# The entry of a one-core decoder trunk: one queue for x and the first two weight tiles, and both tiles taken for each piece of x

## The chip, the cores and the metric

One Trainium2 chip, one core of it. The metric is the device time of one execution in microseconds (us). Three runs of the kernel before gave 826.4, 827.03 and 827.82; their median is 827.03. One further execution was profiled, and all rows of the profile come from it.

TensorE does the matmuls, ScalarE (ACT in rows) and VectorE (DVE) prepare operands and read results, GpSimd (POOL) does small work, and SyncE (SP) issues nearly all transfers.

## The reference, cut to what matters

```python
SEQ, D_MODEL, DEPTH = 256, 1024, 2
for l in range(DEPTH):
    xn = rms_norm(x, norm_mix_g[l])
    proj = xn @ w_in[l]
    xa, q, k, v, zc, xd = jnp.split(proj, splits, axis=-1)
    q = rope(q.reshape(B, S, ATT_HEADS, HEAD_DIM), positions)
    k = rope(k.reshape(B, S, ATT_HEADS, HEAD_DIM), positions)
    ...
    x = x + merged.astype(x.dtype) @ w_o[l]
    hn = rms_norm(x, norm_ffn_g[l])
    gu = hn @ w_ffn_in[l]
    x = x + (jax.nn.silu(gu[..., :FF_DIM]) * gu[..., FF_DIM:]) @ w_ffn_out[l]
return rms_norm(x, final_norm_g)
```

x is 256 tokens by 1024 channels, in float32. Four token mixers (pooling, attention, spatial gating, convolution) stand between `proj` and `merged`; the change does not touch them.

## The kernel before

**Products of two halves.** Every float32 weight tile and every activation is split into a high part (`w_hi`, `act_hi`, a float32r copy made by ScalarE) and a low part (`w_lo`, `act_lo`, the difference, made by VectorE). A product then takes three matmuls: hi x hi, hi x lo, lo x hi. A weight tile ("unit") holds 1 MB. The first units are columns of `w_in`: 1024 rows (8 blocks of 128, called k 0 to 7) by 256 columns. A unit is 48 matmuls of 256 columns: two column halves, eight k, three products.

**The ring.** `RING` is 3: three buffers each of `raw`, `w_hi` and `w_lo`; unit u uses buffer u % 3. SP loads unit u + 3 into `raw` when VectorE has finished the low part of unit u (`lo_ready`); ScalarE copies it to `w_hi` when TensorE has used that buffer (`w_used`), VectorE forms `w_lo`, and TensorE starts on it. Each engine runs its own list of instructions in order; semaphores tie them together.

**The norm.** xn's factor 1/rms does not go into the activations. TensorE works on x times the gains, and the factor is applied to results. ScalarE squares x (`first_norm`), VectorE adds the squares (`square_sum`), TensorE sums over the partitions (`norm_stat`, line 1105, after unit 2 in the first layer), VectorE computes the root and a diagonal (`norm_scale`, lines 1472 to 1476, ready: `diag_ready`), and TensorE spreads it (`norm_rms`, line 1115) after unit 3 and ahead of unit 4.

**The entry**, which the change rewrites. x comes in four pieces x0 to x3 of 256 channels (`load_x`, 256 KB each) and units 0 and 1 in four quarters of two k each (`load_quarter`, 256 KB each; quarter i of unit 0 is called q0i, of unit 1 q1i); unit 2 comes in two halves of 512 KB (lines 489). SP issues q00, x1, q01, x3, q03, then q10 to q13, the halves of unit 2, the positions and `ifreq`. ScalarE's queue issues the gains, x0, x2 and q02. TensorE turns a piece of x by four transposes (`first_x`, line 1252; x0's k 1 is turned a second time into another bank, line 1257), ScalarE multiplies it by the gains into `act_hi` (line 843) and VectorE forms `act_lo` (line 1769). Quarters are split on ScalarE (line 643, a helper that all copies share) and VectorE (line 1751).

TensorE's order before: 34 warm-up matmuls on zeros (`warm`), the turning of the gains (line 1278), x0, x1, 6 warm-ups, k 0 of unit 0, x2, k 1 of unit 0, x3, quarters 1 to 3 of unit 0, all of unit 1, unit 2, and so on. VectorE's order before: q00, x0, x1, q01, q02, x2, q03, x3, q10 to q13, the halves of unit 2, the position steps (lines 1806 to 1812: positions times frequencies, in turns), the sums of squares, the split of unit 3, the split of unit 4, `norm_scale`, `reduce_angles`, the split of unit 5. ScalarE takes the quarters and pieces in the same order, then the squares, one piece of x kept, and the splits of units 3, 4 and 5 as they land.

Lines 967 to 969 and 1012 to 1014 are the three matmuls of a product; line 1433 is VectorE's split of a whole unit, line 429 SP's load of one.

Of the kernel before, what the change touches and what calls it, by code (L numbers as in the profile page):

```python
# [124 lines left out]
def build(nc, T, out, inv_freq, inv_count):  # L125
# [10 lines left out]
    with ExitStack() as ctx:  # L136
# [287 lines left out]
        def _(sp):  # L424
# [51 lines left out]
                else:  # L476
                    load(l, slot, use, down(l, j), n=D)

            load_quarter(sp, 0, 0)
            load_x(sp, 1)  # L480
            load_quarter(sp, 0, 1)
            load_x(sp, 3)
            load_quarter(sp, 0, 3)
            for i in range(4):
                load_quarter(sp, 1, i)
            c0, w_rows = W_IN_UNITS[2][1], T["w_in"][0].rearrange("(k p) n -> p k n", p=P)
            for h, landed in enumerate((half_in, raw_full[2])):
# [140 lines left out]
        def _(act):  # L628
            act.dma_start(gain_rows[0:L * KT, :], T["norm_mix_g"].rearrange("l (r p) -> (l r) p", p=P))\
                .then_inc(gain_in, 16)  # L630
            load_x(act, 0)
            load_x(act, 2)
            load_quarter(act, 0, 2)

            for s in (1, 2):
                act.sem_inc(lo_ready[s], 1)
# [194 lines left out]
            def quarter(u, i):  # L831
# [2 lines left out]
                copy(kview(w_hi[u])[:, 2 * i:2 * i + 2, :], kview(raw[u])[:, 2 * i:2 * i + 2, :])\  # L834
                    .then_inc(quarter_hi[u] if i < 3 else hi_ready[u], 1)

            def first_x(i):
                act.wait_ge(xt_done, i + 1)
                for f in range(2):
                    k = 2 * i + f  # L840
                    if k == 1:
                        act.wait_ge(turned_again, 1)
                    last = nc.scalar.activation(act_hi[:, k, :], first_turned(k), ACT.Copy, scale=gains[:, k:k + 1])
                    if k == 0:
                        last.then_inc(first_hi, 1)
                last.then_inc(act_hi_ready, 1)

            def unit2_halves():
                hi = kview(w_hi[2])
# [5 lines left out]

            act.wait_ge(pre_const, 4)
            copy(junk[:, 0, 0:1], ones[:, 0:1])
            quarter(0, 0)
            act.wait_ge(gains_ready, 1)
            first_x(0)  # L860
            first_x(1)
            quarter(0, 1)
            for i in (2, 3):
                quarter(0, i)
                first_x(i)
            for i in range(4):
                quarter(1, i)
            unit2_halves()

# [94 lines left out]
        def _(pe):  # L964
# [296 lines left out]
            def quarter(u, i):  # L1261
                if i < 3:
                    pe.wait_ge(quarter_lo[u], i + 1)
                else:
                    weights(0, u, 0)
                if (u, i) == (0, 0):
                    pe.wait_ge(first_lo, 1)
                    unit_pair(0, 0, (0,))
                    first_x(2)
                    pe.wait_ge(act_lo_ready, 1)  # L1270
                    return unit_pair(0, 0, (1,))
                return unit_pair(u, u, (2 * i, 2 * i + 1))

            pe.wait_ge(pre_const, 1)
            warm(34)
            pe.wait_ge(pre_const, 3)
            pe.wait_ge(gain_in, 16)
            nc.tensor.transpose(bank[0][:, 0:L * KT], gain_rows[0:L * KT, :], ident[0:L * KT, 0:L * KT])\
                .then_inc(pre_pe, 1)
            first_x(0)  # L1280
            first_x(1)
            warm(6)
            pe.wait_ge(gains_ready, 1)
            for i in range(4):
                if i == 1:
                    first_x(3)
                if i > 0:
                    pe.wait_ge(act_lo_ready, i + 1)
                last = quarter(0, i)
            last.then_inc(w_used[0], 1)  # L1290
            pe.wait_ge(pre_const, 6)

            for l in range(L):
                for u in range(U_WO):
                    if l == 0 and u < 2:
                        if u == 1:
                            for i in range(4):
                                last = quarter(1, i)
                            last.then_inc(w_used[1], 1)
                            misc(l, u)  # L1300
                        continue
                    weights(l, u % RING, u // RING)
                    if u == 7:
# [94 lines left out]
        def _(dve):  # L1398
# [358 lines left out]
            def chain(ins):  # L1757
                turn[0] += 1
                ins.then_inc(turns_chain, 1)
                dve.wait_ge(turns_chain, turn[0])  # L1760

            def first_x(i):
                for f in range(2):
                    k = 2 * i + f
                    if k == 0:
                        dve.wait_ge(first_hi, 1)
                    else:
                        dve.wait_ge(act_hi_ready, i + 1)
                    last = V.scalar_tensor_tensor(act_lo[:, k, :], first_turned(k), gains[:, k:k + 1],
                                                  act_hi[:, k, :].bitcast(F32), ALU.mult, ALU.subtract)  # L1770
                    if k == 0:
                        last.then_inc(first_lo, 1)
                last.then_inc(act_lo_ready, 1)

            def unit2_halves():
                hi, lo, whole = kview(w_hi[2]), kview(w_lo[2]), kview(raw[2])
# [3 lines left out]
                V.tensor_tensor(lo[:, 4:8, :], whole[:, 4:8, :], hi[:, 4:8, :].bitcast(F32), ALU.subtract)\  # L1780
                    .then_inc(lo_ready[2], 1)

            quarter(0, 0)
            first_x(0)
            first_x(1)
            quarter(0, 1)
            for i in (2, 3):
                quarter(0, i)
                first_x(i)
            for i in range(4):  # L1790
                quarter(1, i)
            def reduce_angles():
# [12 lines left out]
            dve.wait_ge(pos_in, 16)  # L1805
            chain(V.tensor_copy(posf[:, 0, :], pos_i))
            dve.wait_ge(ifreq_in, 16)
            chain(V.tensor_scalar(ang[:, 0, :], posf[:, 0, :], ifreq[:, 0:1], None, ALU.mult))
            V.tensor_scalar(turns[:, 0, :], ang[:, 0, :], 1.0 / (2 * np.pi), None, ALU.mult)
            chain(V.tensor_scalar(turns[:, 1, :], ang[:, 0, :], 1.0 / (2 * np.pi), 0.25, ALU.mult, ALU.add))  # L1810
            chain(V.tensor_scalar(turns, turns, magic, None, ALU.add))
            chain(V.tensor_scalar(turns, turns, magic, None, ALU.subtract))
            dve.wait_ge(pre_const, 6)

            for i in range(1, 4):
                square_sum(0, 0, i)

            for l in range(L):
                if l > 0:
# [9 lines left out]
                        square_sum(l, 0, i)  # L1829
                    split(l, 2, 0)  # L1830
                for u in range(U_FFN):
                    if u == 1 + (l == 0):
                        norm_scale(l, 0)
                    if l == 0 and u == 2:
                        reduce_angles()
                    misc(l, u)
                    merge(l, u)
                    if u != U_WO + 2:
                        split(l, (u + 3) % RING, (u + 3) // RING)
# [102 lines left out]
```

## Time and profile before

| What | Value |
|---|---|
| median of 3 runs | 827.03 us (826.4 to 827.82) |
| the profiled execution | 827.67 us |
| its span, first to last instruction | 825.94 us |
| TensorE matmuls busy | 817.6 us of the span |
| VectorE / ScalarE busy | 611.9 / 459.2 us |
| mean rate of the transfers | 189 GB/s |

The device time of an execution is its span and what lies around it, here 1.73 us. Times in rows are us from the start of the span unless marked ns. Matmuls overlap, so that a row of one shows its whole latency, and the step from one to the next is read from the chain of waits.

### The profile page before, as it was taken

The numbers are of one execution on the slowest core, as the hardware profiler recorded it, in microseconds if no ns is written. First come the engines' busy times: TensorE is split into PE (matmuls) and PEld (weight loads), VectorE is DVE, ScalarE is ACT, GpSimd is POOL, SyncE is SP. The second block draws the span as 40 slices with busy tenths as digits, with TensorE's granted clock in tenths as the row PEclk, the third lists the DMA queues.
The fourth block names the chain that finished last, engine by engine and source line by source line (L and its number), as shares of the span: only waits on it lengthen the run. The fifth ranks groups of instructions, "written<-read, shape, count | busy, mean of one in ns | idle before, by whom it ended". The sixth has DMA issues, their size and how long they took to land.

```text
span 825.9 us, 12748 instructions
## 1 busy us (share of the span) xinstructions
PE 817.6 (99%) x4970; PEld 721.7 (87%) x4970; DVE 611.9 (74%) x733; ACT 459.2 (56%) x627; POOL 154.2 (19%) x146
## 2 busy tenths in 40 slices
PE   8999999999999999999999999999999999999997
PEld 8999888888989999999999988878899888888885
DVE  5989788977786666565787898888687667565664
ACT  6656687534564454445465577755355554445544
POOL 2407754083000000000000385523300000000000
PEclk9999999999999999999999999999999999999999
DMA  9965545656545555646468565465645465645451
GB/s 291 314 217 184 165 163 181 226 194 218 186 152 167 192 202 175 223 161 204 155 205 253 167 213 167 151 223 163 215 159 178 152 204 167 223 168 202 156 177 52
DMA packets 103549, 156.17 MB, mean 189 GB/s; under 512 B 4032, under 2 KB 68850, under 8 KB 103504
## 3 DMA queue, kind: packets, MB, share of 16 engines
q1 hardware_dynamic: 101216, 152.71, 55.8%
q0 software_dynamic: 1296, 1.79, 0.8%
q10 hardware_dynamic: 992, 1.06, 0.4%
q8 instruction: 30, 0.49, 0.3%
q14 instruction: 15, 0.12, 0.0%
HBM read 152.39 MB, written 1.05 MB: 186 GB/s over the span
## 4 chain that ended last, share of the span: by engine, by line
PE 96%; DVE 1%; ACT 1%; DMA 1%; issue 0%; ACTq 0%; DVEq 0%
PE bank L1079 19%; PE bank L1081 10%; PE bank L1024 8%; PE bank L1026 8%; PE bank L1025 8%; PE bank L967 8%; PE bank L968 8%; PE bank L969 8%; PE bank L1056 5%; PE bank L1054 5%; PE bank L1055 5%; ACT w_hi L643 1%; PE bank L1164 1%; DMA gates<-in_x 1%; PE bank L1185 1%; DVE w_lo L1433 0%
## 5 line engine op out<-in xcount | busy, mean ns | idle before, releaser
L1433 DVE TENSOR_TENSOR w_lo<-raw,w_hi 128x2048 fp32r<-128x2048 f32 x135 | 318.4, 2360 | 133.8 <-ACT w_hi L643 133.3
L643 ACT ACTIVATE w_hi<-raw 128x2048 fp32r<-128x2048 f32 (+2 forms) x145 | 264.1, 1828 | 131.6 <-PE bank L1026 56.1
L1079 PE MATMUL bank<-act,w_hi 128*128 128x512 f32 x704 | 247.6, 395 | 0.0
L1081 PE MATMUL bank<-act,w_lo 128*128 128x256 f32 x704 | 196.9, 280 | 0.0
L1079 PEld LDWEIGHTS bank<-act,w_hi 128*128 128x128 f32 x704 | 132.0, 188 | 30.3
L1081 PEld LDWEIGHTS bank<-act,w_lo 128*128 128x128 f32 x704 | 132.8, 189 | 0.4
L1024 PE MATMUL bank<-w_hi,act 128*128 128x512 f32 x288 | 114.3, 397 | 0.0
L1026 PE MATMUL bank<-w_hi,act 128*128 128x512 f32 x288 | 112.3, 390 | 0.0
L1025 PE MATMUL bank<-w_lo,act 128*128 128x512 f32 x288 | 112.1, 389 | 0.0
L643 ACT ACTIVATE qk<-bank 128x256 f32<-128x256 f32 (+1 forms) x96 | 37.4, 394 | 76.4 <-PE bank L1081 76.3
L967 PE MATMUL bank<-act,w_hi 128*128 128x256 f32 x256 | 73.6, 287 | 0.2 <-DVE act L1456 0.2
L968 PE MATMUL bank<-act,w_hi 128*128 128x256 f32 x256 | 72.6, 284 | 0.0
L969 PE MATMUL bank<-act,w_lo 128*128 128x256 f32 x256 | 72.5, 283 | 0.0
L1024 PEld LDWEIGHTS bank<-w_hi,act 128*128 128x128 f32 x288 | 54.1, 188 | 11.9 <-issue 1.4
L1026 PEld LDWEIGHTS bank<-w_hi,act 128*128 128x128 f32 x288 | 54.1, 188 | 11.5
L1025 PEld LDWEIGHTS bank<-w_lo,act 128*128 128x128 f32 x288 | 54.2, 188 | 10.7
L581 POOL TENSOR_TENSOR conv_a<-gates,par 128x256 f32<-128x256 f32 x2 | 3.7, 1833 | 293.8 <-ACT gates L810 293.8
L967 PEld LDWEIGHTS bank<-act,w_hi 128*128 128x128 f32 x256 | 49.4, 193 | 0.6 <-DVE act L1456 0.4
L969 PE MATMUL bank<-ff_hi,w_lo 128*128 128x256 f32 x176 | 49.6, 282 | 0.0
L968 PE MATMUL bank<-ff_lo,w_hi 128*128 128x256 f32 x176 | 49.5, 282 | 0.0
L967 PE MATMUL bank<-ff_hi,w_hi 128*128 128x256 f32 x176 | 49.5, 281 | 0.0
L968 PEld LDWEIGHTS bank<-act,w_hi 128*128 128x128 f32 x256 | 49.4, 193 | 0.1
(249 smaller groups left out, 1421.7 us busy)
## 6 DMA issues: line engine op xcount, KB each, us to landing
raw<-in_w_ffn_in SPq DMA_DIRECT2D x44, 1024.0 KB, 5.1
raw<-in_w_gate SPq DMA_DIRECT2D x32, 1024.0 KB, 5.5
raw<-in_w_ffn_out SPq DMA_DIRECT2D x22, 1024.0 KB, 5.0
raw<-in_w_in SPq DMA_DIRECT2D x19, 1024.0 KB, 6.4
raw<-in_w_o SPq DMA_DIRECT2D x8, 1024.0 KB, 5.1
raw<-in_w_proj_b SPq DMA_DIRECT2D x4, 1024.0 KB, 4.9
gates<-qk SPq DMA_DIRECT2D x32, 64.0 KB, 5.1
raw<-in_w_proj_a SPq DMA_DIRECT2D x2, 1024.0 KB, 4.9
```

The source lines that it names most:

```text
L643: return nc.scalar.activation(o, i, ACT.Copy)
L967: nc.tensor.matmul(o, whi, ahi, start=first, stop=False, skip_group_check=skip)
L968: nc.tensor.matmul(o, whi, alo, start=False, stop=False, skip_group_check=skip)
L969: return nc.tensor.matmul(o, wlo, ahi, start=False, stop=last, skip_group_check=skip)
L1024: nc.tensor.matmul(o, act_hi[:, kk, ts], hi[:, k, :], start=(kk == 0), stop=False)
L1025: nc.tensor.matmul(o, act_hi[:, kk, ts], lo[:, k, :], start=False, stop=False)
L1026: last = nc.tensor.matmul(o, act_lo[:, kk, ts], hi[:, k, :], start=False, stop=(kk == KT - 1))
L1054: nc.tensor.matmul(o, y, hi[:, k, cs], start=first and k == 0, stop=False, skip_group_check=True)
L1055: nc.tensor.matmul(o, y, lo[:, k, cs], start=False, stop=False, skip_group_check=True)
L1079: nc.tensor.matmul(bank[b + f], hi[:, k, fs], act2[:, k, :, :].rearrange("p h s -> p (h s)"), start=(k == 0), stop=False, skip_group_check ...
L1081: last = nc.tensor.matmul(main(b)[:, f, :], lo[:, k, fs], act_hi[:, k, :], start=False, stop=(k == KT - 1), skip_group_check=True)
L1433: V.tensor_tensor(w_lo[slot][:, :], raw[slot][:, :], w_hi[slot][:, :].bitcast(F32), ALU.subtract)\
```

## The change

SP issues x0, q00, q10, x1, q01, q11, x2, q02, q12, x3, q03, q13, and ScalarE's queue only the gains. TensorE does k 0 of unit 0 after x0, then turns x1, does k 1 of unit 0 and quarter 0 of unit 1, and from there takes quarter i of both units for each piece of x, each piece being turned one step ahead. The first quarter of unit 0 is split row by row (k 0, then k 1), interleaved with the two rows of x0. The warm-ups are 24 and 8 and not 34 and 6. VectorE's position steps move from ahead of the sums of squares to the loop's u = 1, between the splits of units 3 and 4.

```diff
-            load_quarter(sp, 0, 0)
-            load_x(sp, 1)
-            load_quarter(sp, 0, 1)
-            load_x(sp, 3)
-            load_quarter(sp, 0, 3)
             for i in range(4):
+                load_x(sp, i)
+                load_quarter(sp, 0, i)
                 load_quarter(sp, 1, i)
...
-            load_x(act, 0)
-            load_x(act, 2)
-            load_quarter(act, 0, 2)
...
+            def first_rows():            # ScalarE
+                def w_row(k):
+                    return copy(kview(w_hi[0])[:, k, :], kview(raw[0])[:, k, :])
+
+                act.wait_ge(xt_done, 1)
+                first_k(0).then_inc(first_hi, 1)
+                act.wait_ge(quarter_in[0][0], 16)
+                act.wait_ge(w_used[0], 1)
+                w_row(0).then_inc(first_hi, 1)
+                act.wait_ge(turned_again, 1)
+                first_k(1).then_inc(act_hi_ready, 1)
+                w_row(1).then_inc(quarter_hi[0], 1)
...
-            quarter(0, 0)
             act.wait_ge(gains_ready, 1)
-            first_x(0)
-            first_x(1)
-            quarter(0, 1)
-            for i in (2, 3):
+            first_rows()
+            quarter(1, 0)
+            for i in range(1, 4):
+                first_x(i)
                 quarter(0, i)
-                first_x(i)
-            for i in range(4):
                 quarter(1, i)
             unit2_halves()
...
             pe.wait_ge(pre_const, 1)     # TensorE
-            warm(34)
+            warm(24)
             pe.wait_ge(pre_const, 3)
             pe.wait_ge(gain_in, 16)
             nc.tensor.transpose(bank[0][:, 0:L * KT], gain_rows[0:L * KT, :], ident[0:L * KT, 0:L * KT])\
                 .then_inc(pre_pe, 1)
             first_x(0)
+            warm(8)
+            pe.wait_ge(gains_ready, 1)
+            pe.wait_ge(first_lo, 1)
+            unit_pair(0, 0, (0,))
             first_x(1)
-            warm(6)
-            pe.wait_ge(gains_ready, 1)
-            for i in range(4):
-                if i == 1:
-                    first_x(3)
-                if i > 0:
-                    pe.wait_ge(act_lo_ready, i + 1)
-                last = quarter(0, i)
-            last.then_inc(w_used[0], 1)
+            pe.wait_ge(act_lo_ready, 1)
+            pe.wait_ge(quarter_lo[0], 1)
+            unit_pair(0, 0, (1,))
+            quarter(1, 0)
+            for i in range(1, 4):
+                if i < 3:
+                    first_x(i + 1)
+                pe.wait_ge(act_lo_ready, i + 1)
+                last = [quarter(u, i) for u in range(2)]
+            last[0].then_inc(w_used[0], 1)
+            last[1].then_inc(w_used[1], 1)
...
+            def first_rows():            # VectorE
+                def w_row(k):
+                    return V.tensor_tensor(kview(w_lo[0])[:, k, :], kview(raw[0])[:, k, :],
+                                           kview(w_hi[0])[:, k, :].bitcast(F32), ALU.subtract)
+
+                dve.wait_ge(first_hi, 1)
+                first_k(0)
+                dve.wait_ge(first_hi, 2)
+                w_row(0).then_inc(first_lo, 1)
+                dve.wait_ge(act_hi_ready, 1)
+                first_k(1).then_inc(act_lo_ready, 1)
+                dve.wait_ge(quarter_hi[0], 1)
+                w_row(1).then_inc(quarter_lo[0], 1)
...
+            def position_steps():
+                dve.wait_ge(pos_in, 16)
+                chain(V.tensor_copy(posf[:, 0, :], pos_i))
...
                 for u in range(U_FFN):
+                    if l == 0 and u == 1:
+                        position_steps()
                     if u == 1 + (l == 0):
                         norm_scale(l, 0)
```

VectorE's order of quarters and pieces changes as ScalarE's does, and `position_steps` holds the same seven steps as before, removed from their place behind `unit2_halves()`.

## Rows read from the trace of the kernel before

**Rows 1.** The page: busy time, and the issues of one kind of load (count, size, median to landing).
```profile
PE 817.6 (99%) x4970; PEld 721.7 (87%) x4970; DVE 611.9 (74%) x733; ACT 459.2 (56%) x627; POOL 154.2 (19%) x146
...
raw<-in_w_ffn_in SPq DMA_DIRECT2D x44, 1024.0 KB, 5.1
```
**Rows 2.** The waits of TensorE over the span: us in total, times, longest.
```profile
PE bank L1252 <- DMA gates<-in_x: 1.2, 1, 1.2
```
**Rows 3.** TensorE's timeline at the entry: start, time, what [idle before, releaser].
```profile
1.07 3.81 PE L1245 MATMUL bank<-zeros 128*128 128x128 bf16 x34 [1.07 <-POOL zeros L544]
4.81 0.28 PE L1278 MATMUL bank<-ident,gain_rows 16*128 16x16 f32 x1
6.34 1.12 PE L1252 MATMUL bank<-ident,gates 128*128 128x128 f32 x4 [1.25 <-DMA gates<-in_x]
...
9.13 0.56 PE L967 MATMUL bank<-act,w_hi 128*128 128x256 f32 x1
```
**Rows 4.** The chain that ended last, 9 to 36 us: start, us, what.
```profile
10.12 0.21 PE bank L967
10.34 0.12 PE bank L968
...
10.59 0.44 PE bank L1252 x4
...
28.00 0.34 PE bank L1105 x4
...
34.20 0.44 PE bank L1115 x4
```
**Rows 5.** SP's timeline: when it issues transfers.
```profile
0.81 0.45 SPq L391 DMA_DIRECT2D raw<-in_w_in  x1
...
1.82 0.47 SPq L391 DMA_DIRECT2D raw<-in_w_in  x1
...
13.91 5.82 SPq L429 DMA_DIRECT2D raw<-in_w_in  x3
```
**Rows 6.** Issues from 0.8, 1.8 and 13.9 us: size, us to landing.
```profile
raw<-in_w_in SPq DMA_DIRECT2D x1, 256.0 KB, 3.1
...
raw<-in_w_in SPq DMA_DIRECT2D x1, 256.0 KB, 5.3
...
raw<-in_w_in SPq DMA_DIRECT2D x1, 1024.0 KB, 6.6
```
**Rows 7.** ScalarE's timeline.
```profile
7.55 0.84 ACT L843 ACTIVATE act<-bank,gains 128x256 fp32r<-128x256 f32 x2 [1.94 <-PE bank L1252]
...
12.20 0.63 ACT L643 ACTIVATE w_hi<-raw 128x512 fp32r<-128x512 f32 x1
...
16.92 1.06 ACT L643 ACTIVATE w_hi<-raw 128x1024 fp32r<-128x1024 f32 x1 [0.30 <-DMA raw<-in_w_in]
...
20.54 1.92 ACT L643 ACTIVATE w_hi<-raw 128x2048 fp32r<-128x2048 f32 x1
```
**Rows 8.** VectorE's timeline, 8 to 34 us.
```profile
8.06 0.88 DVE L1769 SCALAR_TENSOR_TENSOR act<-bank,gains,act 128x256 fp32r<-128x256 f32 x2 [1.65 <-ACT act L843]
...
13.13 0.68 DVE L1751 TENSOR_TENSOR w_lo<-raw,w_hi 128x512 fp32r<-128x512 f32 x1
...
19.20 0.28 DVE L1806 CAST gates<-gates 128x256 f32<-128x256 int32 x1
...
21.36 2.15 DVE L1464 TENSOR_TENSOR sq<-sq 128x512 f32<-128x512 f32 x3
...
23.88 4.49 DVE L1433 TENSOR_TENSOR w_lo<-raw,w_hi 128x2048 fp32r<-128x2048 f32 x2
28.38 0.16 DVE L1472 TENSOR_SCALAR st<-bank 128x2 f32<-128x2 f32 x1
...
30.82 0.69 DVE L1798 SCALAR_TENSOR_TENSOR angles<-gates 128x512 f32<-128x512 f32 x1
...
33.86 2.29 DVE L1433 TENSOR_TENSOR w_lo<-raw,w_hi 128x2048 fp32r<-128x2048 f32 x1
```
**Rows 9.** Stretches: PE, PEld, DVE, ACT, POOL busy, granted clock, DMA share, GB/s.
```profile
4.00:6.00 2.00, 1.09 (x10) 0.79 (x7) 0.45 (x2) 1.60 (x3) 0.00 (x0) 1.00 0.84 226
...
9.00:15.00 6.00, 6.00 (x50) 6.00 (x48) 4.83 (x10) 5.18 (x13) 0.00 (x0) 1.00 1.10 358
```

More of the change, by code:

```diff
@@ L835, in quarter, with first_k @@
                     .then_inc(quarter_hi[u] if i < 3 else hi_ready[u], 1)
+            def first_k(k):
+                return nc.scalar.activation(act_hi[:, k, :], first_turned(k), ACT.Copy, scale=gains[:, k:k + 1])
             def first_x(i):
                 act.wait_ge(xt_done, i + 1)
[L839 to L846, printed above, removed]
+                first_k(2 * i)
+                first_k(2 * i + 1).then_inc(act_hi_ready, 1)
+            def first_rows():
[9 more added lines that the diff above has]
+                w_row(1).then_inc(quarter_hi[0], 1)
             def unit2_halves():
@@ L1265, in quarter @@
                     weights(0, u, 0)
[L1266 to L1271, printed above, removed]
                 return unit_pair(u, u, (2 * i, 2 * i + 1))
             pe.wait_ge(pre_const, 1)
-            warm(34)
+            warm(24)
             pe.wait_ge(pre_const, 3)
@@ L1295, in _ @@
                     if l == 0 and u < 2:
[L1296 to L1300, printed above, removed]
                         continue
@@ L1760, in chain, with first_k @@
                 dve.wait_ge(turns_chain, turn[0])
+            def first_k(k):
+                return V.scalar_tensor_tensor(act_lo[:, k, :], first_turned(k), gains[:, k:k + 1],
+                                              act_hi[:, k, :].bitcast(F32), ALU.mult, ALU.subtract)
             def first_x(i):
[L1763 to L1773, printed above, removed]
+                dve.wait_ge(act_hi_ready, i + 1)
+                first_k(2 * i)
+                first_k(2 * i + 1).then_inc(act_lo_ready, 1)
+            def first_rows():
[10 more added lines that the diff above has]
+                w_row(1).then_inc(quarter_lo[0], 1)
             def unit2_halves():
@@ L1781, in unit2_halves @@
                     .then_inc(lo_ready[2], 1)
[L1783 to L1787, printed above, removed]
+            first_rows()
+            quarter(1, 0)
+            for i in range(1, 4):
+                first_x(i)
                 quarter(0, i)
-                first_x(i)
-            for i in range(4):
                 quarter(1, i)
+            def position_steps():
+                dve.wait_ge(pos_in, 16)
+                chain(V.tensor_copy(posf[:, 0, :], pos_i))
+                dve.wait_ge(ifreq_in, 16)
+                chain(V.tensor_scalar(ang[:, 0, :], posf[:, 0, :], ifreq[:, 0:1], None, ALU.mult))
+                V.tensor_scalar(turns[:, 0, :], ang[:, 0, :], 1.0 / (2 * np.pi), None, ALU.mult)
+                chain(V.tensor_scalar(turns[:, 1, :], ang[:, 0, :], 1.0 / (2 * np.pi), 0.25, ALU.mult, ALU.add))
+                chain(V.tensor_scalar(turns, turns, magic, None, ALU.add))
+                chain(V.tensor_scalar(turns, turns, magic, None, ALU.subtract))
+                dve.wait_ge(pre_const, 6)
             def reduce_angles():
@@ L1804, in _ @@
             unit2_halves()
[L1805 to L1813, printed above, removed]
             for i in range(1, 4):
```

## The prediction

> **What bounds the kernel now.** The page comes first: TensorE is busy for 817.6 of 825.9 us [rows 1]. So time is saved only by letting its real work start earlier, and only if nothing later makes it wait for what was saved. The list of waits shows TensorE waiting for one transfer, 1.2 us for the first piece of x [rows 2]; all else it waits for is start-up. TensorE's timeline shows the entry: warm-up matmuls from 1.07, the turning of the gains at 4.81, x turned from 6.34, the first real matmul at 9.13 [rows 3]. The chain shows no hole after that: unit 2 ends at 28.00, norm_stat follows, unit 3 runs to 34.20, norm_rms takes 0.44, and unit 4 starts at 34.64 [rows 4]. (Units 0 and 1 are the first two weight tiles.) TensorE is the chain from 9.13 on, so unit 4's start measures the whole change: what it gains there stays, since the order of later work is the same. Everything below is compared at that point.
>
> **Start of the first matmul.** Before, q00 (quarter 0 of unit 0) was issued first on SP, at 0.81, and landed 3.1 us later, at 3.9 [rows 5, 6]; x0 went out on ACT's queue and released TensorE only at 6.34 [rows 3]. Now x0 has q00's place, with the same 256 KB, so I take 3.9 for it (not before 3.4: the same transfer without a competitor could save some of its 0.8 us; not after 6.3). The warm-up is cut from 34 to 24, which took 3.81 us for 34: its end moves from about 4.7 to 3.7, the gains are turned (0.28), and x0's transposes start at 4.0. From there the chain is that of before: ScalarE starts on x at 7.55, 1.21 after TensorE's start [rows 3, 7], so 5.2; VectorE 0.51 behind it [rows 7, 8], so 5.7. New here are the single rows of weights, 128x256, on both engines. No row has them in this form; above, one costs no more than the 128x512 one (0.68 on VectorE [rows 8]), below, half of it. I take 0.42, half of the 0.84 of two ScalarE pieces of 128x256 [rows 7]. ScalarE: x row 0 to 5.6, weight row 0 to 6.05; VectorE: x row 0 to 6.15, weight row 0 to 6.6. The weights for it are the second load of the queue; three loads of 256 KB had landed by 6.3 and four by 7.1 (q01, issued 1.82, landing in 5.3) [rows 3, 5, 6], so the second lies near 5. First real matmul: 6.65. **Saved 2.5 us** (1.9 to 2.9). The warm(8) ends at about 6.4 and is hidden in this wait.
>
> **What moves behind it.** The four transposes of x1, which lay ahead of the first matmul, now follow it. At the high clock four take 0.44 (those of x2 and x3 did, within the unbroken chain [rows 4]). **Lost 0.44.**
>
> **The clock.** Matmuls of 256 columns step at 0.21 us up to 10.3 and at 0.12 from there, which are the 1.2 and 2.4 GHz levels [rows 4]; TensorE had worked without a hole since 6.34, while the work from 1.07 to 5.1 with a hole of 1.25 behind it had not raised it [rows 3]. Now the holes are about 0.3 us at 3.7 and 0.3 at 6.4, so the clock may be up by 6.65. Before, the first six matmuls took 9.13 to 10.59, 1.46 us instead of 0.72 [rows 3, 4]. **Saved 0.5**, between nothing and 0.74.
>
> **One queue instead of two.** The transfers are bound by their sum: 358 GB/s between 9 and 15 us, but 226 between 4 and 6 [rows 9]. The sum of bytes is unchanged, so the last half of unit 2 lands as before, at 16.9 [rows 7]. Per piece of x TensorE now has 24 matmuls and four transposes, 24 x 0.12 + 0.44 = 3.3 us, for 768 KB, which take 2.3 us at the steady rate. x1 is the fourth load and lands by 7.1; it is wanted at 7.4 to 7.9, behind the first six matmuls. VectorE needs for a piece 0.88 + 2 x 0.68 = 2.2 us [rows 8]: hidden under 3.3. Cost nothing; if the rate stayed at 226 GB/s the third rival below would begin. Unit 2: its halves are split one behind the other, 1.06 us each on ScalarE [rows 7]: the second half, landed at 16.9, is through ScalarE at 18.1 and through VectorE (1.2 more) at 19.4. TensorE wants it at 25.5 - 5.76 = 19.7. Hidden by 0.3, the thinnest cover of the entry.
>
> **What becomes late: unit 3 and the norm.** Unit 3's tile goes into unit 0's buffer, and SP issues it when the low half of q03 is done: 13.91 before, landing in 6.6 [rows 5, 6, 8]. Now unit 0 ends together with unit 1. Call E the end of TensorE's work on quarter 1 of unit 1. From E to the end of unit 2 it has four transposes, four quarters (12 matmuls of 0.12 each) and unit 2 (48): 0.44 + 4 x 1.44 + 5.76 = 11.96. Unit 2 now ends at 28.00 - 2.5 + 0.44 - 0.5 = 25.5, so E is 13.5. x3's transposes come behind E (0.44), ScalarE's x and q03 (0.09 + 0.84 + 0.63), VectorE's q03 (0.1 + 0.6): E + 2.7 = 16.2, 2.3 us later than before. The load: 5.1 us, the median of the 44 loads of this size in the FFN [rows 1]; the 6.6 of before is the upper bound, as it was issued 3.0 us ahead of the landing of unit 2's second half (16.9 [rows 7]), which went before it; now that is 0.6. Lands 21.4. ScalarE splits it (1.92), VectorE (2.29) from 23.4: **unit 3 ready at 25.6**; TensorE wants it at 25.8. Just in time; before it was ready at 26.1 for 28.34 [rows 8].
>
> The position steps, on VectorE ahead of the sums of squares (19.20 to 21.36, 2.16 us [rows 8]), now stand behind unit 3's split, and so ahead of unit 4's split (2.25) and norm_scale (28.38 to 30.82, 2.44). TensorE needs norm_scale's diag at the end of unit 3. VectorE: 25.6 + 2.16 + 2.25 + 2.5 = 32.5, with hand-over 32.7. TensorE: 25.8 + 5.86 = 31.7. It waits 1.0 us where it had 3.3 to spare (30.9 against 34.20 [rows 4, 8]). Both times hang on E, so the wait is the same when the start comes out otherwise: E + 19.2 against E + 18.2. **Lost 1.0** (nothing if the load takes 4.1; 2.5 if it takes 6.6). The move of the steps costs its 2.16 there, but at its old place it would have found VectorE free between 19.4 and 23.4, so it is the move that makes this wait. Behind it, reduce_angles (30.82 to 33.86) and unit 5's split end at about 38.0, wanted at 38.9: hidden. ScalarE's rotary tables and unit 6 follow by 41, wanted at 45.
>
> **A rule against the trace.** Rows first: a 1 MB load takes 5.1 us from issue to landing in the FFN [rows 1]. The Trainium skill, "DMA: Bandwidth & Descriptors", section "Anatomy of one DMA", fits about 2.0 us plus bytes at 436 GB/s for loads from GpSimd's queue, 4.4 us for 1 MB; its section on issuing engines says that loads of either queue share the same 16 engines, with which the steady 358 GB/s agree. By 4.4 the wait would be 0.3 us and the sum 2.2. I go by 5.1.
>
> **Sum.** 2.5 - 0.44 + 0.5 - 1.0 = 1.5 us saved, unit 4 starting at 33.1. Against the profiled execution's own 827.67 (span 825.94) that is 826.1; it lies 0.64 above the median of the three runs, 827.03, so for the median **825.5**. A measurement of this kernel tells 0.2% (1.65 us) from nothing: the forecast stands just inside.
>
> **Rivals.**
> 1. *No wait at norm_rms*: the load lands in 4.4 or VectorE's chain is shorter, or the clock is up early and its whole 0.74 counts. Saved 2.2 to 2.6: 824.6. For it: E may come earlier than ScalarE's part needs; against it: 5.1 is a median of many loads. The page's 4.4 belongs here. Chance 0.40, with the upper part of the forecast's own spread.
> 2. *The load of unit 3 as slow as before*, 6.6: wait at unit 3 and norm_rms 2.5 in all, saved 0.0: 827.0. For it: it is the one row of this very load; against it: the 3.0 us of other transfers ahead of it then. Chance 0.17.
> 3. *The single queue starves TensorE* (slower): at the 226 GB/s of 4 to 6 us kept up, 4 MB need 18.6 us and not the 13 to 14 of before, unit 2's second half lands at 21 instead of 16.9, TensorE waits 4 us at unit 2 and unit 3's load is pushed behind it by as much: 829.5. It decides from a landing after 20.2, that is below some 235 GB/s on average. Against it: the 358 GB/s of 9 to 15 us [rows 9], when SP's queue carried most. Chance 0.08.
> 4. *The forecast*, a wait of about 1 us: 825.5, own range 824.6 to 826.4. Chance 0.35.
>
> The range takes in the first two and the forecast: 824.0 (start 0.4 earlier, full clock gain, no wait) to 827.2. Faster by over 0.2% is below 825.4: all of rival 1 and a fourth of the forecast, 0.49. Within 0.2%: the rest of the forecast and rival 2, 0.42. Slower 0.09.
>
> **What would show it.** First real matmul (L967 of before) near 6.65 and not 9.13; steps of 0.12 us from the first on; x0 landing near 3.9; no wait of TensorE for x1 to x3; unit 2 ending at 25.5; unit 3's load issued near 16.3, landing near 21.4; VectorE's position steps right behind unit 3's split; a TensorE wait of about 1 us on VectorE's diag ahead of norm_rms; unit 4 starting at 33.1. It is wrong if x0 lands at 5 or later, if TensorE waits on the halves of unit 2, or if unit 4's start and the end differ by more than the 791.3 us that now lie between them.

## The result

The changed kernel takes 828.42 us in the median of 20 runs (828.02 to 830.17), the kernel before 827.46 in 20 (826.4 to 828.72): a ratio of 1.0015, interval 1.0008 to 1.0021. So it is slower by about 1 us, where 1.5 us less were forecast (825.5, range 824.0 to 827.2). The ratio is built on the average of all runs and not on the two medians. The profiled execution of the changed kernel took 828.39 us, with a span of 826.6.

The entry did what it was meant to. TensorE's timeline in the changed kernel (start, time, what, idle before and releaser), to be held against [rows 3]:

```profile
3.82 0.25 PE L1273 MATMUL bank<-ident,gain_rows 16*128 16x16 f32 x1
4.22 1.04 PE L1253 MATMUL bank<-ident,gates 128*128 128x128 f32 x4
...
5.32 0.61 PE L1246 MATMUL bank<-zeros 128*128 128x128 bf16 x8
6.92 0.36 PE L968 MATMUL bank<-act,w_hi 128*128 128x256 f32 x1 [0.99 <-DVE w_lo L1769]
...
25.74 0.50 PE L1106 MATMUL bank<-ones,sq 128*128 128x1 f32 x4
26.66 0.39 PE L968 MATMUL bank<-act,w_hi 128*128 128x256 f32 x1 [0.42 <-DVE w_lo L1429]
...
33.65 0.68 PE L1116 MATMUL bank<-diag,ones 128*128 128x128 f32 x4 [0.97 <-DVE diag L1472]
...
40.96 0.20 PE L1126 MATMUL bank<-ident,gain_rows 16*128 16x16 f32 x1 [0.89 <-issue]
```

The first real matmul starts at 6.92 and not 9.13, and norm_stat (25.74; in this timeline 27.84 before) is 2.1 us earlier. Then TensorE waits three times, for things it did not wait for before: 0.42 at unit 3, 0.97 at norm_rms, and 0.89 ahead of the turning of the parameters, a step behind unit 4 (small tensors of norm gains and other parameters) that the prediction did not look at. The advance is 2.1 us at norm_stat, 0.4 at norm_rms (33.65 against 34.04), and at the parameters it is a loss of 0.64 (40.96 against 40.32). From there both programs run alike, 785.6 us to the end in either. The list of TensorE's waits (us in total, times, longest) says the same:

```profile
PE bank L968 <- DVE w_lo L1769: 1.0, 1, 1.0
PE bank L1116 <- DVE diag L1472: 1.0, 1, 1.0
PE bank L1126 <- issue: 0.9, 1, 0.9
PE bank L968 <- DVE w_lo L1429: 0.4, 1, 0.4
```

The first line is the wait for the first weights, which only ends the warm-up. "Issue" in the third means that the list names no releaser. The code names one: the parameters are turned into bank 6 (`bank_wait(l, 6, "par")`), which holds the norm's factor until ScalarE has copied it (`rms_copy`). ScalarE's timeline:

```profile
14.42 0.84 ACT L832 ACTIVATE act<-bank,gains 128x256 fp32r<-128x256 f32 x2 [1.61 <-PE bank L1253]
...
22.36 1.92 ACT L637 ACTIVATE w_hi<-raw 128x2048 fp32r<-128x2048 f32 x1 [1.73 <-DMA raw<-in_w_in]
...
36.89 0.42 ACT L719 ACTIVATE sin_r<-angles 128x256 f32<-128x256 f32 x1 [1.57 <-DVE angles L1817]
...
37.70 1.92 ACT L637 ACTIVATE w_hi<-raw 128x2048 fp32r<-128x2048 f32 x1
...
40.48 0.39 ACT L637 ACTIVATE rms_b<-bank 128x256 f32<-128x256 f32 x1
```

The copy ends at 40.87 and TensorE goes on at 40.96. It stands behind the rotary tables, which wait 1.57 us for VectorE's angles, and behind the split of unit 6. In the kernel before it ran at 38.22, and TensorE came at 40.32 (rows of before, ScalarE and TensorE):

```profile
38.22 0.38 ACT L643 ACTIVATE rms_b<-bank 128x256 f32<-128x256 f32 x1
40.32 0.23 PE L1125 MATMUL bank<-ident,gain_rows 16*128 16x16 f32 x1
```

VectorE's timeline of the changed kernel shows the order that the prediction gave, [rows 8] moved:

```profile
16.09 1.28 DVE L1747 TENSOR_TENSOR w_lo<-raw,w_hi 128x512 fp32r<-128x512 f32 x2
...
24.31 2.29 DVE L1429 TENSOR_TENSOR w_lo<-raw,w_hi 128x2048 fp32r<-128x2048 f32 x1 [2.15 <-ACT w_hi L637]
26.52 0.28 DVE L1797 CAST gates<-gates 128x256 f32<-128x256 int32 x1
...
28.78 2.29 DVE L1429 TENSOR_TENSOR w_lo<-raw,w_hi 128x2048 fp32r<-128x2048 f32 x1
...
33.02 0.48 DVE L1472 TENSOR_SCALAR diag<-ident,rms_t 128x128 f32<-128x128 f32 x2
```

Unit 3 is split from 24.31, the steps follow from 26.52, unit 4's split from 28.78, the diag at 33.02. Unit 3 is late because its load could be issued only when the low half of q03 was done; SP's timeline and the issue's time to landing (5.5 us):

```profile
16.87 3.24 SPq L429 DMA_DIRECT2D raw<-in_w_in  x3
```
```profile
raw<-in_w_in SPq DMA_DIRECT2D x1, 1024.0 KB, 5.5
```

### The profile page after: what moved, and what is told of

It reads as the page before. It is cut to its first block, busy times and chain, and to the rows that moved or that the text cites. A ratio compares the mean times of both kernels' runs of the same rounds, so it can differ in the third digit from the quotient of the medians.

```text
span 826.6 us, 12734 instructions
## 1 busy us (share of the span) xinstructions
PE 816.0 (99%) x4962; PEld 719.6 (87%) x4962; DVE 612.4 (74%) x734; ACT 459.5 (56%) x628; POOL 152.8 (18%) x146
## 4 chain that ended last, share of the span: by engine, by line
PE 94%; DVE 2%; ACT 2%; DMA 1%; issue 1%; DVEq 0%; ACTq 0%; SPq 0%
PE bank L1080 19%; PE bank L1082 10%; PE bank L1025 8%; PE bank L1027 8%; PE bank L1026 8%; PE bank L968 7%; PE bank L969 7%; PE bank L970 7%; PE bank L1057 5%; PE bank L1056 5%; PE bank L1055 5%; ACT w_hi L637 1%; DVE w_lo L1429 1%; DMA raw<-in_w_in 1%; PE bank L1165 1%
## 5 line engine op out<-in xcount | busy, mean ns | idle before, releaser
L637 ACT ACTIVATE w_hi<-raw 128x2048 fp32r<-128x2048 f32 (+3 forms) x146 | 264.0, 1816 | 128.9 <-PE bank L1027 55.7
L1080 PEld LDWEIGHTS bank<-act,w_hi 128*128 128x128 f32 x704 | 132.0, 187 | 30.2
L968 PEld LDWEIGHTS bank<-act,w_hi 128*128 128x128 f32 x256 | 49.1, 192 | 2.3 <-issue 1.1
L637 ACT ACTIVATE ff_hi<-qk 128x512 fp32r<-128x512 f32 x22 | 13.9, 632 | 63.8 <-DVE qk L1729 63.8
```

Of the source, the lines that this page charges most:

```text
L637: return nc.scalar.activation(o, i, ACT.Copy)
L968: nc.tensor.matmul(o, whi, ahi, start=first, stop=False, skip_group_check=skip)
L1080: nc.tensor.matmul(bank[b + f], hi[:, k, fs], act2[:, k, :, :].rearrange("p h s -> p (h s)"), start=(k == 0), stop=False, skip_group_check ...
```

## The experiments

Theory A, formed on these rows: three waits stand one behind the other, each from a delay of its own (unit 3's tile, the position steps on VectorE, the norm's factor copied late on ScalarE), and taking one away shows the next. All times are medians; ratios are against runs of the kernel before from the same comparison (median 827.37 to 827.54), with their interval. The names in the first column are those of the sections below. The columns "clock", "norm_stat" and "parameters" come from the one profile of each kernel: when TensorE's clock rose, and when TensorE started on the two steps. "The clock rose" means that the steps between matmuls changed from 0.21 us (1.2 GHz) to 0.12 us (2.4 GHz); where no matmul of 256 columns shows it, the shorter warm-ups and transposes do. The granted clock of such a stretch reads 1.00 ahead of the rise too, because the trace has no clock record before it.

A profile with a late rise reads some 1.3 to 1.6 us later at norm_stat, so rows are compared with rows of the same kind.

| Kernel | clock | norm_stat | parameters | us | ratio |
|---|---|---|---|---|---|
| before | 10.2 | 27.84 | 40.32 | 827.46 | |
| changed | 5.1 | 25.74 | 40.96 | 828.42 | 1.0015 (1.0008 to 1.0021) |
| steps late alone | 4.0, and again 10.9 | 27.91 | 40.39 | 827.34 | 0.9998 (0.9989 to 1.0007) |
| steps back | 10.4 | 27.30 | 42.14 | 829.69 | 1.0029 (1.0016 to 1.0041) |
| factor first | 9.6 | 27.19 | 41.17 | 827.8 | 1.0004 (0.9995 to 1.0013) |
| steps back, factor first | 5.6 | 25.87 | 38.85 | 826.22 | 0.9988 (0.9979 to 0.9997) |
| last quarters first | 5.9 | 25.87 | 38.73 | 827.36 | 1.0 (0.9991 to 1.001) |
| last quarters and factor first | 5.8 | 25.81 | 38.80 | 825.95 | 0.9986 (0.9977 to 0.9994) |
| the same, steps behind norm_scale | 5.4 | 25.80 | 38.28 | 826.03 | 0.9986 (0.9977 to 0.9995) |
| the same, holes filled | 4.5 | 25.60 | 38.08 | 825.84 | 0.9981 (0.9972 to 0.999) |
| changed, 4 warm-ups | 9.5 | 27.09 | 42.70 | 829.6 | 1.0024 (1.0015 to 1.0033) |
| changed, x on ScalarE's queue | 9.7 | 27.76 | 42.88 | 830.54 | 1.0038 (1.0024 to 1.0052) |
| before, hole filled | 3.8 | 27.40 | 39.88 | 827.2 | 0.9997 (0.9988 to 1.0006) |

### The steps late, alone

```diff
 # on the kernel before, VectorE
-            dve.wait_ge(pos_in, 16)
-            chain(V.tensor_copy(posf[:, 0, :], pos_i))
...
                 for u in range(U_FFN):
+                    if l == 0 and u == 1:
+                        position_steps()
```

> The kernel before with one part of the change alone: VectorE's position steps stand between the splits of units 3 and 4. The point compared is the turning of the parameters after unit 4, at 40.32 us before and 40.96 in the changed kernel. Theory A (the order: the steps cost only where TensorE comes earlier): VectorE splits unit 3 from 22.5, does the steps to 27.0, unit 4's split to 29.2, norm_scale's diag to 31.8, 2.4 us ahead of norm_rms at 34.2; the angles are ready some 0.8 us later than at 33.9, and ScalarE has to wait for unit 6's tile until 35.4 anyhow. No wait of TensorE, 40.3, time within 0.1% of before. Rival B (the moved steps alone make the kernel slower): a wait of TensorE at norm_rms or at the parameters already here, 0.6 us or more, ratio 1.001 or above.

827.34 us, no difference. VectorE's diag came at 31.57, over 2 us ahead of norm_rms at 34.11, and nothing of TensorE's waits is new. The whole list:

```profile
PE bank L1252 <- DMA gates<-in_x: 1.9, 1, 1.9
PE bank L1245 <- POOL zeros L544: 1.1, 1, 1.1
PE bank L967 <- DVE act L1456: 0.2, 1, 0.2
```

So the move of the steps costs nothing by itself, and rival B in its plain form falls. (The clock rose at 4.0 here, fell at 7.5, behind the hole of 1.9 us ahead of x0, and rose again at 10.9; from 7.5 to 10.5 the granted clock reads 0.50.)

### The steps back, in the changed kernel

```diff
             unit2_halves()
+            position_steps()
             for i in range(1, 4):
                 square_sum(0, 0, i)
...
-                    if l == 0 and u == 1:
-                        position_steps()
```

> The changed kernel with the position steps back at their old place, ahead of the sums of squares. Theory A (three waits in a row, each hiding behind the one before): norm_rms no longer waits (1.0 us in the changed kernel), since the diag is ready near 31.3 and TensorE comes at 32.4; but ScalarE cannot start on unit 6's split before its tile has landed at 37.7, and copies the norm's factor, which frees the bank that the parameters go to, only behind that split, near 40.9. So the wait ahead of the parameters grows from 0.9 to about 2.0 us, they are turned at 40.9 as in the changed kernel, and the time is the changed kernel's, 1.0010 to 1.0015 of before. Rival B (the steps' new place is what costs): the whole 1.0 us at norm_rms comes back and the wait at the parameters shrinks with it, 39.0 to 39.9, 0.9985 to 1.0000.

The waits of this kernel:

```profile
PE bank L1126 <- issue: 1.8, 1, 1.8
...
PE bank L968 <- DVE w_lo L1429: 0.3, 1, 0.3
```

The wait at norm_rms is gone and the one at the parameters has grown from 0.9 to 1.8, as theory A has it and against rival B, for which it had to shrink: ScalarE had the angles (its sine ran at 36.67 without waiting) and now waited for unit 6's tile.

```profile
38.88 1.92 ACT L637 ACTIVATE w_hi<-raw 128x2048 fp32r<-128x2048 f32 x1 [1.49 <-DMA raw<-in_w_in]
...
41.65 0.39 ACT L637 ACTIVATE rms_b<-bank 128x256 f32<-128x256 f32 x1
```

The time, 829.69 us (1.0029), is above what was expected (1.0010 to 1.0015), so this expectation missed. In this profile all of the excess lies ahead of norm_stat, 27.30 against 25.74: the clock rose late.

```profile
7.16 0.55 PE L968 MATMUL bank<-act,w_hi 128*128 128x256 f32 x1 [0.38 <-DVE w_lo L1769]
...
10.07 0.41 PE L968 MATMUL bank<-act,w_hi 128*128 128x256 f32 x1
10.28 0.36 PE L969 MATMUL bank<-act,w_hi 128*128 128x256 f32 x1
10.48 0.28 PE L970 MATMUL bank<-act,w_lo 128*128 128x256 f32 x1
10.60 0.28 PE L968 MATMUL bank<-act,w_hi 128*128 128x256 f32 x1
```

Starts lie 0.21 us apart up to 10.28 (1.2 GHz) and 0.12 from 10.48 (2.4 GHz); in the changed kernel's profile the chain steps by 0.12 from the first matmuls on:

```profile
7.27 0.12 PE bank L969
```

Of this kernel's six times five are at 829.43 or above and one is at 828.07, which is where the faster runs of the changed kernel lie. If the five rose late, as the profiled one did, the time is explained; why most of six should do so is not.

### The factor first, alone and with the steps back

```diff
 # ScalarE
                     if l == 0 and u == 3:
+                        rms_copy(l, 0)
                         tables()
...
-                if u == 2 + (l == 0):
+                if u == 2 and l > 0:
                     rms_copy(l, 0)
```

> The changed kernel with one move on ScalarE: in the first layer it copies the norm's factor out of its bank ahead of the rotary tables and of unit 6's split, and not behind them. Theory A: the wait of 0.9 us ahead of the parameters goes, the 0.4 at unit 3 and the 1.0 at norm_rms stay; parameters turned at 40.0, time 0.9 us below the changed kernel, 1.0000 to 1.0006 of before. Rival C (what holds TensorE there is the parameter rows or the FFN gains arriving late, not the bank): the wait stays, 40.96, 1.0015.

> The changed kernel with both moves: steps back at the old place, and the norm's factor copied first. Theory A: neither norm_rms nor the parameters wait; left is the 0.4 us at unit 3 (its tile lands at 22.3 and is split by 26.6). Parameters turned at 38.8 to 39.0, 1.4 us below before, 0.9982 of it (0.9975 to 0.9988). Rival D (the later landings of units 3, 5 and 6, each some 2 us later than before, go on holding TensorE at units 5 or 6): a wait for VectorE's split appears there, the gain of 38.9 is lost again by 60 us, ratio 0.9995 or above.

With the factor first, no wait for the parameters is left and the one at norm_rms stays (its list of waits, first line); with both, that goes too and only unit 3's stays (second):

```profile
PE bank L1117 <- DVE diag L1473: 1.0, 1, 1.0
```
```profile
PE bank L969 <- DVE w_lo L1430: 0.3, 1, 0.3
```

It was the bank, and not the rows of parameters or the gains (rival C). The medians are 827.8 (1.0004, as expected) and 826.22 (0.9988, at the upper end of the expectation). The times of the first lie in two groups, six from 826.75 to 827.8 and five from 828.32 to 828.81; its profile, 828.62, is of the late kind and has no wait at unit 3, since TensorE came 1.5 us later to it. In the second the parameters are turned at 38.85, as expected, and no wait for a later unit appears, so rival D falls too.

### The last quarters first

```diff
 # ScalarE and VectorE alike
-            for i in range(1, 4):
+            for i in range(1, 3):
                 first_x(i)
                 quarter(0, i)
                 quarter(1, i)
+            quarter(0, 3)
+            quarter(1, 3)
+            first_x(3)
```

> The changed kernel with one other order on ScalarE and VectorE: the last quarters of units 0 and 1 are split ahead of the last piece of x and not behind it. Both engines sit idle there (1.6 and 1.4 us) until TensorE has turned x3. Theory A (what makes unit 3 late is that unit 0's buffer comes free late): SP issues unit 3's load near 14.7 and not 16.9, it lands by 20.0, unit 3 is ready at 24.8; the waits at unit 3 (0.4) and at norm_rms (1.0) both go, though the position steps stay at their new place. The wait for the bank of the parameters stays, since the norm's factor is still copied behind unit 6's split (near 39.3), about 1.1 us of it. Parameters turned at 39.5, some 0.9 to 1.1 us below before, ratio 0.9989 (0.9981 to 0.9996). Rival B (the position steps are the cause at norm_rms, wherever unit 3's tile is): the wait at norm_rms stays above 0.5 us. Rival E (the queue is full anyway, so an earlier issue lands no earlier): unit 3's tile lands at 22 still, 1.0015.

SP now issues unit 3's load at 14.72 (first line, SP's timeline), and of the three new waits TensorE's list has only the one ahead of the parameters, 0.3 us (second line; 1.1 were expected):

```profile
14.72 4.46 SPq L429 DMA_DIRECT2D raw<-in_w_in  x3
```
```profile
PE bank L1129 <- issue: 0.3, 1, 0.3
```

The tile landed 5.8 us later, at 20.5, and VectorE split it from 22.47 and not 24.31. The steps stood at their new place, right behind that split, and nothing waited at unit 3 or norm_rms. So unit 3's wait comes from its late tile. The wait at norm_rms needs both the late tile and the steps behind it: with the tile earlier it goes though the steps stay (here), and with the steps back it goes though the tile stays late (steps back, factor first). The profiled execution took 825.94, but the median is 827.36, and so the ratio is 1.0 where 0.9989 (at most 0.9996) was expected. The times spread from 825.94 to 830.15, wider than any other kernel's. What spreads them was not found.

### Both, and the steps behind norm_scale

The second has this edit on top:

```diff
-                    if l == 0 and u == 1:
-                        position_steps()
...
                     if l == 0 and u == 2:
+                        position_steps()
                         reduce_angles()
```

> The same, and ScalarE copies the norm's factor ahead of the rotary tables. Theory A: no wait of TensorE between its first matmul and the parameters, which are turned near 38.5; the whole start advance arrives, 1.8 to 2.0 us below before where the clock rises early, ratio 0.9977 (0.9970 to 0.9986). Rival D (a later tile holds TensorE further on): ratio 0.9988 or above, as in the run with the steps back and the factor first.

> The same again, with the position steps moved one place further, behind norm_scale and ahead of reduce_angles, so that VectorE has unit 4 split by 27 and the diag ready by 29.5 and not 31.7. Theory A: norm_rms had some 0.4 us to spare already, so nothing more is won: within 0.05% of the run before this one, 0.9977. Where the clock rises late, TensorE comes later still and it is hidden as well.

825.95 and 826.03 us, 0.9986 both, at the upper end of what was expected (0.9970 to 0.9986) and not the 0.9977 of its middle. The first still had the wait below (first line): its unit 3 was issued at 14.65 but took 6.5 us and landed at 21.2. The whole list of the second has none behind the first matmul that the kernel before does not have; VectorE's diag was ready at 29.9 there, against 32.3, but unit 3 also landed sooner, at 20.2:

```profile
PE bank L1120 <- DVE diag L1476: 0.3, 1, 0.3
```
```profile
PE bank L1250 <- POOL zeros L541: 1.1, 1, 1.1
PE bank L972 <- DVE w_lo L1773: 0.9, 1, 0.9
PE bank L972 <- DVE act L1456: 0.2, 1, 0.2
PE bank L1257 <- DMA gates<-in_x: 0.2, 1, 0.2
```

The whole advance at norm_stat, 2.0 us, now is there at the end: a span of 823.9 against 825.9. In the medians it is 1.5. The profiled executions are not the medians: this one is the fastest of its 11 runs, of which four lie in an upper group (826.99 to 827.22). The next runs ask what that group is.

### The clock at the entry

```diff
             pe.wait_ge(pre_const, 1)
-            warm(24)
+            warm(4)
```

> The changed kernel with 4 warm-up matmuls at the start and not 24. In the runs so far of kernels with the changed entry the clock rose at 5.1 and 5.6 in two profiles and at 9.6 and 10.4 in two others; at the late rise TensorE's real work began on 0.21 us steps and unit 2 ended 1.5 us later. Theory F (the early rise is owed to the long first stretch of warm-ups, and misses in some executions because of the holes behind it): with 4 the rise always comes late, near 9.5 to 11; unit 2 ends near 27.3 and the time is 0.9 to 1.5 us above the changed kernel's 828.4, 829.3 to 829.9. Rival G (the level at the entry is worth nothing, since the later waits absorb it): 828.4 as with 24.

829.6 us, 1.2 above the changed kernel: with 4 warm-ups the 0.21 us steps last until 9.5, norm_stat comes at 27.09, and the same three waits follow (1.3, 1.0 and 0.4 us). That is what theory F expected, and rival G (828.4) falls. Of the changed kernel's 20 times 15 lie between 828.02 and 828.51 and five between 829.05 and 830.17, where those of the 4 warm-ups lie (828.99 to 830.29). It fits that the clock rises late in some executions; only profiles show it. The Trainium skill, "TensorE: Matmul & The Clock Gate", section "Part 1: The HAM clock gate", says that the same kernel sees the rise at different matmuls from run to run. These traces agree as far as they go: seven kernels, one profile each, have the changed kernel's warm-ups and loads, and the clock rose between 5.1 and 5.9 us in five of them and at 9.6 and 10.4 in two.

The next two fill TensorE's holes with warm-ups, in the best kernel so far and in the kernel before:

```diff
 # on the last one
                 .then_inc(pre_pe, 1)
+            warm(3)
             first_x(0)
-            warm(8)
+            warm(14)
```
```diff
 # on the kernel before
-            warm(34)
+            warm(46)
```

> The kernel with the last quarters first, the norm's factor first and the steps behind norm_scale, and with 3 warm-ups more between the turning of the gains and x0 and 14 instead of 8 behind x0, so that TensorE has hardly a hole from 1.1 us on. Theory F (the holes decide whether the clock rises early): no execution is left in the upper group near 827.2, the median falls from 826.03 to 825.6 to 825.8. Rival (the rise falls where it falls, whatever is done in the holes): two groups as before, median 826.0 or, by the 0.1 to 0.3 us that x0's transposes come later, 826.2.

> The kernel before with 46 warm-ups and not 34, which fill the hole of 1.5 us between the turning of the gains and the landing of x0 (6.3). Theory F: the clock is up before x0 is turned, its transposes and the first matmuls run on 0.12 us steps, the first matmul comes near 8.6 and unit 2 ends near 27.0 and not 27.9: 0.7 to 1.0 us below before, 0.9990. Rival: no change, 1.0000.

The first: 825.84, a little above the 825.6 to 825.8 expected, with all 11 times between 825.28 and 826.6, where the kernel without the filling had four at 826.99 to 827.22. No run of an upper group is among them. By chance alone that would be rare, but it isn't excluded: in four kernels with these holes unfilled (changed; steps back, factor first; last quarters and factor first; steps behind norm_scale) 13 of 53 runs lie in an upper group, and 11 runs without one would then come 1 time in 20, as an estimate. This kernel has the lowest median, 0.19% below before, though its interval overlaps with those of three others. Its first real matmul:

```profile
6.67 0.36 PE L972 MATMUL bank<-act,w_hi 128*128 128x256 f32 x1 [0.66 <-DVE w_lo L1774]
```

The second brought the first matmul from 9.13 to 8.64, with the clock up from 3.8 us on, but norm_stat only to 27.40, 0.4 us earlier, and the median, 827.2, cannot be told from 827.37 in the same comparison. At least half of what was expected did not come. TensorE ran into two waits for VectorE's low part of x, which the kernel before does not have (its list, first line). The first, 0.25 us, is ahead of the first matmul. The second, at 12.90, goes back to a transfer: ScalarE waited for q02, issued on its own queue behind x0 and x2, which landed at 10.56, 8.2 us after its issue, and it takes the third piece of x only behind q02 (second line):

```profile
PE bank L967 <- DVE act L1769: 0.5, 2, 0.3
```
```profile
10.58 0.63 ACT L643 ACTIVATE w_hi<-raw 128x512 fp32r<-128x512 f32 x1 [0.99 <-DMA raw<-in_w_in]
```

So the old entry had little room for an earlier TensorE.

### Two queues

```diff
             for i in range(4):
-                load_x(sp, i)
                 load_quarter(sp, 0, i)
...
                 .then_inc(gain_in, 16)
+            for i in range(4):
+                load_x(act, i)
```

> The changed kernel with the four pieces of x on ScalarE's queue and the quarters on SP's. The whole advance of the first matmul is thought to come from x0 going alone ahead of all else. Theory A: here q00, q10 and q01 share the 16 engines with x0 to x3, x0 lands near 5.5 to 6.3 and not 4.2, the first matmul comes near 8.3 to 8.9 and not 6.9, and nothing behind it gets earlier: 0.8 to 1.6 us above the changed kernel, 829.2 to 830.0. Rival H (the second queue doesn't hurt, as the sum of bytes is the same): 828.4 or below.

830.54 us, beyond the expected range, and the transposes of x0 start at 5.56 and not 4.22:

```profile
5.56 1.11 PE L1254 MATMUL bank<-ident,gates 128*128 128x128 f32 x4 [1.53 <-DMA gates<-in_x]
...
8.33 0.55 PE L969 MATMUL bank<-act,w_hi 128*128 128x256 f32 x1 [0.38 <-DVE w_lo L1770]
```

The second queue brought nothing in (the second half of unit 2 landed at 16.1, and at 16.2 in the changed kernel) and took the first piece's lead away. Of the 1.3 us by which x0 landed later, 0.5 is its place behind the gains on ScalarE's queue (issued at 1.30 and not 0.81) and 0.8 its slower landing (4.2 us and not 3.4), with the first two quarters issued beside it on SP's. The Trainium skill, "DMA: Bandwidth & Descriptors", section "Issuing engines are not separate DMA queues", says that transfers of different queues interleave on the same 16 engines and that a second one only saves time at issue. The slower landing agrees with it; the run does not separate sharing from other causes. The first matmul comes 1.4 us later and norm_stat 2.0, as the clock rose only at 9.7, behind a hole of 1.5 us ahead of x0.

## Why the prediction was wrong

- **Start of the first matmul**: right. 6.92 for 6.65, saved 2.2 for 2.5. x0 landed 3.4 us after its issue at 0.81, so at 4.2 for 3.9. The single rows of weights took 0.41 on both engines (0.42 taken).
- **The clock**: the 0.5 came out in this profile: the first six matmuls took 0.79 us (6.92 to 7.71), and 1.29 before (9.13 to 10.42). The 1.46 of the prediction sets a start from the timeline (9.13) against one from the chain (10.59) and is too large. But the early rise was taken as likely from single profiles. It comes late in part of the executions, and the 4 warm-ups show its price, 1.2 us.
- **x1's transposes**: right, 0.43 for 0.44 (with the first matmul behind them).
- **One queue**: right for the transfers; no wait for x or for unit 2 that was not there before. VectorE's part, "Cost nothing", was 0.2 short: behind x1's piece TensorE's transposes start at 10.30 and the next matmul at 10.84, 0.54 later, where the other pieces have 0.35. VectorE had started the low part of q01 at 10.01, behind x1's, for which ScalarE had to wait until TensorE had turned x1. No run took this away.
- **Unit 3**: the mechanism was right and its sizes too small. SP's issue came 3.1 us behind E and not 2.7 (VectorE has to do x3 before q03, and I had counted ScalarE's part alone), the load took 5.5 and not 5.1. Ready at 26.5, not 25.6, and so a wait where "just in time" was put at nothing. The Trainium skill's fit ("DMA: Bandwidth & Descriptors", section "Anatomy of one DMA") gives an estimate of 4.4 us for such a load, which is lower still; the measurement decides.
- **norm_rms**: right, 0.97 us for 1.0.
- **The step that failed** is "what it gains there stays", said of unit 4's start, and the sentence that was to secure it: "ScalarE's rotary tables and unit 6 follow by 41, wanted at 45". The split of unit 6 was indeed in time. But ScalarE's order has, behind it, the copy of the norm's factor, and TensorE needs that copy's bank for the parameters at 40.1. I asked when unit 6's weights are wanted and not what stands in ScalarE's list behind the instruction that now waited. It cost 1.0 us (0.9 in the list), and with the factor copied first it is gone (factor first; steps back and factor first). The prediction's own sign showed it: unit 4's start and the end lie 1.0 us further apart than before.
- **The sum at unit 4** failed as well: TensorE starts on unit 4 at 34.08 for 34.40 before (timeline), 0.3 us earlier and not 1.5. The first matmul gave 0.3 less, q01 cost 0.2, unit 3 0.6 and norm_rms 0.2 more than was put down.
- **The base**: the forecast went from the median of three runs, 827.03; that of 20 is 827.46, so 0.4 us of the distance from 825.5 to 828.42 is this.

In starts of TensorE the account closes. To norm_stat: 2.2 (start) + 0.5 (clock) - 0.43 (x1) - 0.19 (q01) = 2.1. From there the three waits cost 0.56, 1.15 and 1.03 us, which makes the loss of 0.64 at the parameters. The list says 0.42, 0.97 and 0.89 for them, as it counts from the end of the matmul ahead, and without a wait the next one would have begun before that end. The spans then differ by 0.7 and the medians by 0.96; most of the difference is that the profiled execution of before (827.67) lies 0.2 above its median. Of the rivals none had this form: rival 2 had the load alone as slow as before (6.6; it was 5.5), rival 3 the queue.

## What to carry to other kernels

An advance at the start of a kernel bound by one engine is worth only what the helpers' order of work lets through: each engine that works to a written order has to be followed to its next hand-over, past the instruction that one was thinking of. When a change gives several new waits in a row, taking one away can show nothing (steps back: 1.0 us less at norm_rms, 0.9 more at the parameters), and no kernel was faster than before with the bank's wait or the one at norm_rms still whole. And a buffer is freed by the last reader in the helper's order, so moving two splits into an idle gap ahead of them let a 1 MB load go out 2.1 us earlier, and TensorE did not wait for that piece of x.

## What the runs showed of the hardware

TensorE's clock rose at 5.1 us in one profile and at 10.4 in another of kernels with the same entry. With TensorE's holes of the first 6 us filled it rose at 4.5 in the profile, and the 11 times lay within 1.3 us. That the holes decide it in each execution was not shown, since only profiles tell when the clock rose. In one profile of the old entry (steps late alone) it rose at 4.0 and fell back at 7.5, behind a hole of 1.9 us, and norm_stat came no earlier for it (27.91); in another (before, hole filled) it rose at 3.8 and stayed up over a hole of 1.5 us.

A load of 256 KB, issued first on SP's queue with only the 8 KB of gains on the other, took 3.4 us to land, against 3.1 for the first load of the kernel before, with x0 and x2 on the second queue behind the gains: no faster for having the second queue empty. The load of unit 3 (1 MB) took less when it was issued later: 6.6 to 7.7 us when issued at 13.5 to 13.9, 5.6 to 6.5 at 14.3 to 14.7, and 5.2 to 5.5 at 16.9 to 18.9, by which time unit 2's second half had landed (16.2 in the changed kernel). So of 2.1 us by which a load is issued earlier, not all arrives (last quarters first: landing 1.8 us earlier; the next kernel: 1.2).
